# Layer B of a hybrid decoder step: keys and values turned by VectorE and on-chip transfers instead of by TensorE

## The reference

```python
qkv = h @ w_in[:, :3072]                      # 1024 tokens
conv = silu(sum(xpad[:, w:w + T] * conv_w[w] for w in range(4)))
q, k, v = split(conv)                         # (T, 8 heads, 128)
q, k = l2norm(q) * SCALE, l2norm(k)
kb   = k * beta
lmat = strict_lower(kb @ k.T) * decay         # in each chunk of tokens
sol  = triangular_solve(lmat, [v * beta, kb * exp(gc)])     # unit diagonal
u, w = sol
aqk  = (q @ k.T) * decay
kdec = k * exp(g_last - gc)
# chunk after chunk:
v_new = u - w @ S
o     = (q * exp(gc)) @ S + aqk @ v_new
S     = S * exp(gl) + kdec.T @ v_new
```

## Time and profile before

| | us |
|---|---|
| median of three runs | 2113.65 |
| the profiled execution: its own time | 2113.68 |
| the profiled execution: span from first to last instruction | 2111.6 |
| TensorE busy in the span | 2072.5 (98%) |
| VectorE, ScalarE, GpSimd busy | 997.2, 697.7, 454.6 |

### The profile page before, as it was taken

How to read it: one execution, slowest core, us unless ns; L and a number is a source line. 1 busy time by engine, 2 the same in 40 slices (tenths; PEclk the granted TensorE clock), 3 DMA queues, 4 the chain that set the end, 5 groups by cost and what they waited for, 6 DMA issues and landing times. The chain is left out here.

```text
span 2111.6 us, 36594 instructions
## 1 busy us (share of the span) xinstructions
PE 2072.5 (98%) x14446; PEld 1487.2 (70%) x14446; DVE 997.2 (47%) x2664; ACT 697.7 (33%) x1631; POOL 454.6 (22%) x639
## 2 busy tenths in 40 slices
PE   8999999999999999999999999999999999999998
PEld 6888888888888887555466777767666666665444
DVE  5234354354435345331238777777876133332252
ACT  4121321322131122231135555555564344532101
POOL 0522232222223213300023134322331200020000
PEclk9999999999999999999999999999998999999999
DMA  7411301211131127668412122222210461134451
GB/s 235 161 43 41 107 27 51 80 41 43 41 97 37 50 83 223 237 202 255 131 31 74 73 95 83 93 87 82 73 48 13 137 256 31 41 105 134 134 161 50
DMA packets 210238, 210.34 MB, mean 100 GB/s; under 512 B 14261, under 2 KB 181653, under 8 KB 209150
## 3 DMA queue, kind: packets, MB, share of 16 engines
q1 hardware_dynamic: 198070, 148.27, 23.7%
q0 software_dynamic: 12000, 59.73, 7.4%
HBM read 179.56 MB, written 68.23 MB: 117 GB/s over the span
## 5 line engine op out<-in xcount | busy, mean ns | idle before, releaser
L887 PE MATMUL bank<-arena 128*128 128x256 f32 (+1 forms) x2688 | 631.7, 386 | 0.0
L887 PEld LDWEIGHTS bank<-arena 128*128 128x128 f32 x2688 | 494.5, 190 | 75.3
L2104 PE MATMUL bank<-arena 128*128 128x352 f32 x1296 | 452.5, 470 | 0.1
L2104 PEld LDWEIGHTS bank<-arena 128*128 128x128 f32 x1296 | 220.8, 191 | 71.4 <-issue 1.0
L2909 PE MATMUL bank<-arena 128*128 128x352 f32 x576 | 176.4, 459 | 0.0
L3399 PE MATMUL bank<-arena 128*128 128x512 f32 x360 | 167.5, 599 | 0.0
L2162 PEld LDWEIGHTS bank<-arena 128*128 128x128 f32 x864 | 129.9, 194 | 45.7 <-DVE arena L2646 3.7
L2909 PEld LDWEIGHTS bank<-arena 128*128 128x128 f32 x576 | 106.6, 190 | 53.3
L1341 POOL TENSOR_TENSOR arena<-arena 128x272 f32<-128x272 f32 (+1 forms) x48 | 31.5, 656 | 507.4 <-ACT arena L1061 487.4
L2162 PE MATMUL bank<-arena 128*128 128x128 f32 x864 | 135.0, 280 | 1.5 <-DVE arena L2646 1.0
L1323 POOL TENSOR_TENSOR arena<-arena 128x512 f32<-128x512 f32 x96 | 122.8, 1279 | 11.3 <-POOL arena L1323 0.9
(11 more groups left out here) (432 smaller groups left out, 2754.1 us busy)
## 6 DMA issues: line engine op xcount, KB each, us to landing
arena<-in_w_in_a SPq DMA_DIRECT2D x48, 512.0 KB, 5.2
arena<-in_w_in_b SPq DMA_DIRECT2D x40, 512.0 KB, 7.5
arena<-in_cache_win_k SPq DMA_DIRECT2D x48, 256.0 KB, 6.1
arena<-in_cache_win_v SPq DMA_DIRECT2D x48, 256.0 KB, 4.7
out<-arena SPq DMA_DIRECT2D x40, 256.0 KB, 3.4
arena<-in_w_mem_kv SPq DMA_DIRECT2D x16, 512.0 KB, 8.1
arena<-in_cache_mem_k SPq DMA_DIRECT2D x32, 256.0 KB, 4.3
arena<-in_cache_mem_v SPq DMA_DIRECT2D x32, 256.0 KB, 4.2
```

The source lines that it names most:

```text
L887: m = nc.tensor.matmul(o[:, 0:hi - lo], w, y, start=k == 0 and i in (0, 1, 3, 5), stop=k == KH - 1, skip_group_check=i in (2, 4, 6))
L2104: m = nc.tensor.matmul(bank[j % 3][:, 0:PART], ring.slots[:, (B1 + b) % RING, k, :], part_in(k, part_), start=k == 0, stop=k == KD - 1)
```

## The change

VectorE turns the keys and the values inside 32x32 blocks by its stream transpose, one instruction of 128x512 each for k and v of a group (`kv_turned`); SyncE then issues 16 transfers for a group (`turned_to`), each of 32 partitions by 256 words (32 KB), that move the blocks between the quarters of the partitions and so complete the turn; ScalarE reads the result chunk by chunk and scales it into `kdec` and `vb` (`scale_turned`, two activations of 128x128 for a chunk, in slots 2 to 5 of iteration G for group G). VectorE's part for group G+1 is in slots 6 and 7 of iteration G; for group 0 it stands ahead of the loop. The steps "kt" and "vt" and their read-outs are gone. SyncE's order of weight loads is written anew around the transfers. In iteration 15 the four extra units move from slots 0 to 3 to slots 12 to 15. The buffers are parts of tensors that are free in this stage; the waits that guard them are in the diff. (The class `Chain` takes another way to its semaphore, which changes no instruction of the work.)

```diff
@@ names
+    turned_in = [brT[:, HB - 2, 0:1024]] * (2 * HB - 1) + [xpad[:, 0, 0:1024]]
+    turned_kv = [w.rearrange("p (b i c x) -> p b i c x", b=4, i=2, c=4) for w in turned_in]
+    kv_words = sb[:, ZM[0]:ZM[0] + 1024]
+    kv_back = kv_words.rearrange("p (a i c x) -> p a i c x", a=4, i=2, c=4)
-    PREP = {5: ("ra",), 7: ("kt",), 8: ("kk",), 9: ("qk",), 15: ("vt",)}
+    PREP = {5: ("ra",), 8: ("kk",), 9: ("qk",)}
+    AT_TURN = {6: 0, 7: 1}
+    SCALE_AT = {2: 0, 3: 1, 4: 2, 5: 3}
-    slots += [[(0, 1)] * 16, [(0, 2)] * 4 + [(0, 1)] * 12]
+    slots += [[(0, 1)] * 16, [(0, 1)] * 12 + [(0, 2)] * 4]
@@ SyncE
+        def turned_to(g):
+            sp.wait_ge(turnd, 2 * (g + 1))
+            after(sp, kvs, 4 * g)
+            for b in range(4):
+                for a in range(4):
+                    sp.dma_start(kv_words[quarter(b), 256 * a:256 * a + 256],
+                                 turned_in[g][quarter(a), 256 * b:256 * b + 256]).then_inc(kv_in[g % 2], 16)
+        for b in range(7):
+            weights(b)
+        turned_to(0)
+        for G in range(NG_):
+            if G % 2 and G < NG_ - 1:
+                weights(3 * (G // 2) + 8)
+                weights(3 * (G // 2) + 9)
+            if G + 1 < NG_:
+                turned_to(G + 1)
+            if G % 2 == 0:
+                weights(3 * (G // 2) + 7)
@@ TensorE
-                readout(pe, g, f"ks{c}" if c else "vt")
+                if c:
+                    readout(pe, g, f"ks{c}")
+                else:
+                    pe.wait_ge(kvs, 4 * g + 1)
+                pe.wait_ge(kvs, 4 * g + cl + 1)
                 to(g, f"su{c}", [(kdec[:, c, :], vn[:, c % 2, :])])
-            elif name == "kt":
-                to(G, "kt", [(ch(k_, c), None) for c in cs])
-            elif name == "vt":
-                to(G, "vt", [(ch(v, c), None) for c in cs])
@@ ScalarE
+        def scale_turned(g, cl):
+            w, c = hd[:, g // 2 % 2], GR[g % 2][0] + cl
+            if not cl:
+                act.wait_ge(kv_in[g % 2], 256 * (g // 2 + 1))
+                act.wait_ge(hdv, 3 * g + 3)
+                if g > 1:
+                    left(act, g - 2, f"su{GR[g % 2][1] - 1}")
+            wide = lambda v: v.rearrange("p (a x) -> p a x", x=32)
+            nc.scalar.activation(wide(kdec[:, c, :]), kv_back[:, :, 0, cl, :], ACT.Copy, scale=w[:, KD_, c:c + 1])
+            nc.scalar.activation(wide(vb[:, c, :]), kv_back[:, :, 1, cl, :], ACT.Copy,
+                                 scale=w[:, KN, c:c + 1]).then_inc(kvs, 1)
...
+                if G < NG_ and s in SCALE_AT:
+                    scale_turned(G, SCALE_AT[s])
                 for u in ended(units_at(G, s)):
                     piece(*u)
@@ VectorE
-            elif name == "kt":
-                dve.wait_ge(hdv, 3 * G + 3)
-                nc.vector.tensor_tensor(kdec[:, cs, :], bk(b), factors_of[:, KD_, cs]...)
-            elif name == "vt":
-                nc.vector.tensor_tensor(vb[:, cs, :], bk(b), factors_of[:, KN, cs]...)
+        def kv_turned(G, i):
+            h, gr = G // 2, G % 2
+            dve.wait_ge(sild, 3 * G + 2 + i)
+            if G and not i:
+                dve.wait_ge(kv_in[(G - 1) % 2], 256 * ((G + 1) // 2))
+            if G == NG_ - 1 and not i:
+                dve.wait_ge(cvd, 3 * NG_)
+                dve.wait_ge(tap, 3 * (NG_ - 2))
+            x = qkvT[:, h % 2, 1 + i, gr * 512:(gr + 1) * 512].rearrange("p (c b x) -> p c b x", c=4, b=4)
+            nc.vector.transpose(turned_kv[G][:, :, i].rearrange("p b c x -> p c b x"), x).then_inc(turnd, 1)
...
         turned(0, "qk")
+        kv_turned(0, 0)
+        kv_turned(0, 1)
         for w in range(CW):
             conv(1, 2, w)
...
                     chunk_step(G - 1, s)
+                if s in AT_TURN and G + 1 < NG_:
+                    kv_turned(G + 1, AT_TURN[s])
```

More of the change, by code:

```diff
@@ L115, with __init__ @@
 class Chain:
-    def __init__(self, nc, eng, name):
-        self.eng, self.sem, self.n = eng, nc.alloc_semaphore(name), 0
+    def __init__(self, sem, eng, name):
+        self.eng, self.sem, self.n = eng, sem(name), 0
     def __call__(self, ins):
@@ L525, in _ @@
     def _(dve):
-        own = Chain(nc, dve, "in_dve")
+        own = Chain(sem, dve, "in_dve")
         def norm(n):
@@ L1130, in _ @@
     def _(dve):
-        own = Chain(nc, dve, "dve_a")
+        own = Chain(sem, dve, "dve_a")
         def evacuate(t, i):
@@ L1300, in _ @@
     def _(pool):
-        own = Chain(nc, pool, "pool_a")
+        own = Chain(sem, pool, "pool_a")
         def weight_sums(pair, ns):
@@ L1747, in _ @@
     def _(dve):
-        own = Chain(nc, dve, "wa_dve")
+        own = Chain(sem, dve, "wa_dve")
         def add(n, half):
@@ L2000, in build @@
     (pd, pr_, wk, rd_act, rd_dve, cvd, sild, sqd, hdv, hda, exd, mt0, onm, sqo, fac, tails, sqrt_o, cstep, xzero,
-     cvs, spread, base, tap, chosen) = (
+     cvs, spread, base, tap, chosen, turnd, kv_even, kv_odd, kvs) = (
         sem(f"b_{n}") for n in (
@@ L2005, in build @@
             "out_factors", "conv_tails", "out_roots", "conv_steps", "buffers_zeroed", "samples_convolved",
-            "diagonals_spread", "base_steps", "first_taps", "blocks_chosen"))
+            "diagonals_spread", "base_steps", "first_taps", "blocks_chosen",
+            "kv_turned", "kv_moved_even", "kv_moved_odd", "kv_scaled"))
+    kv_in = (kv_even, kv_odd)
     s_out = stored["state"]
@@ L2078, in state_away, with weights @@
             sp.dma_start(p_delta[0, 0, h], S_of(h, NT)).then_inc(s_out, 16)
-        for b in range(3 * HB):
+        def turned_to(g):
[5 more added lines that the diff above has]
+                                 turned_in[g][quarter(a), 256 * b:256 * b + 256]).then_inc(kv_in[g % 2], 16)
+        def weights(b):
             if b % 3 == 2 and b // 3 >= 3:
@@ L2313, in gate_piece @@
                 act.wait_ge(ring.used, B2 + i + 1)
+            if i == 1 and part_ == 0:
+                act.wait_ge(kvs, 4 * NG_)
             if i == 2 and part_ == 0:
@@ L2390, in outputs @@
             b = left(act, g, "ot")
+            if g == 2 * (HB - 2):
+                act.wait_ge(kv_in[0], 256 * HB)
             nc.scalar.activation(brT[:, g // 2, g % 2 * 512:(g % 2 + 1) * 512], b[:, :], ACT.Copy,
                                  scale=onw).then_inc(rd_act, 1)
+        def scale_turned(g, cl):
[9 more added lines that the diff above has]
+                                 scale=w[:, KN, c:c + 1]).then_inc(kvs, 1)
         def choose_blocks(G):
@@ L2489, in _ @@
     def _(dve):
-        own = Chain(nc, dve, "b_dve")
+        own = Chain(sem, dve, "b_dve")
         stepped = [0]
@@ L2643, in chunk_step @@
             if x == "a" and c:
-                readout(dve, g, "vt")
+                dve.wait_ge(kvs, 4 * g + cl + 1)
                 b = left(dve, g, f"ks{c}")
@@ L2772, in _ @@
     def _(pool):
-        own = Chain(nc, pool, "b_pool")
+        own = Chain(sem, pool, "b_pool")
         def prefix(h, i):
@@ L3009, in _ @@
     def _(dve):
-        own = Chain(nc, dve, "m_dve")
+        own = Chain(sem, dve, "m_dve")
         def conv_turned(t):
@@ L3487, in _ @@
     def _(act):
-        own = Chain(nc, act, "d_act_own")
+        own = Chain(sem, act, "d_act_own")
         def squared(o):
@@ L3558, in _ @@
     def _(dve):
-        own = Chain(nc, dve, "wb_dve")
+        own = Chain(sem, dve, "wb_dve")
         gt2 = lambda v: v[:, 64:66].unsqueeze(2)
```

6 lines of the change are left out of this document (removed).

## The result

The changed kernel takes **2338.4 us** (median of 4 runs, 2336.44 to 2338.97) against 2112.92 (4 runs, 2111.94 to 2114.21) of the kernel before on the same chip: a ratio of 1.1065, interval 1.1046 to 1.1084. The forecast was 2107.1, in a range of 2099 to 2115. It was wrong, and by a cause that it had priced at nothing.

What follows compares the result with a forecast made beforehand. TensorE, busy 2072.5 of 2111.6 us, was taken to bound the kernel; -10.3 (steady) + 2.6 (iteration 0) - 0.1 (13, 14) + 1.2 (15) = -6.6 from 2113.7 gave 2107.1 us, range 2099 to 2115.

Steps and rivals of the forecast that it cites:

- The transfers in those iterations: Iterations 1 to 12: last landing 14 us after VectorE's second turn (bounds 7.2, 17.3), hidden in 24.6 us: 0.
- The slower rival: Each group's 16 transfers run one after another, 29.8 us against 24.6 of room: 3.7 lost per group, 2162; 8 in 100.
- Steady iterations: Iterations 1 to 12: TensorE spared 24 turns at 0.43 us, -10.3 us (bounds 5.2 and 10.3 gained).
- The exponentials' chain: Rival, steady part: ScalarE's added scalings delay exponentials and VectorE's kk read-out, losing half of 10.3: 2112.3 us; 13 in 100.
- Iteration 0: First loop iteration: ScalarE waits for transfers landing at 1128, x4 +3.0 us, "vt" returns 0.43: +2.6 (bounds +1.0, +4.6).
- The first group's stall and the clock: Rival, iteration 0: x4 5.0 us late, then a half-clock stretch; -6.6 + 2.0 + 5.6 gives 2114.7 us; 13 in 100.
- Iterations 13 and 14: Late iterations where units run out: almost nothing gained, half clock counted as it was: -0.1 us (bounds -1.7, +1.0).
- Iteration 15: Last iteration: moved units and ScalarE's scalings make TensorE stand 1.7 us more, less 0.43: +1.2 (bounds -0.9, +2.6).

Runs made afterwards that it cites:

- the half transfers: Changed kernel, cache copies as they were, each of the 16 transfers carrying 128 of 256 words a partition: 2337.02 us (one run).
- the copies spread: Changed kernel with each two-row cache copy written as two one-row copies, each seen as 16 pieces: 2110.56 us, ratio 0.9989 to the kernel before.

## Why the prediction was wrong, step by step

**The step that failed** is "The transfers in those iterations", priced at 0 because landing 14 us behind the turn, at worst 17.3, would be hidden in a room of 24.6. The room was right, and in quiet the landing too (11 to 14 us). The bound was not: beside a copy the first group's last transfer landed 44 us behind the turn, and the later ones up to 59. It came from the stores of a state, 11.6 us at most, and from the median of the weight loads, 9.9. A median over loads that meet a copy and loads that don't is no bound, and the trace of before had the right number one view further on. The weight loads by line, from 1106 to 1560 us, in the kernel before:

```profile
L139 SPq DMA_DIRECT2D arena<-in_w_in_b x20: 367/368/2649, 1144.7 to 1559.0; - x20
...
DMA to landing us min/median/max: 4.1/10.8/43.5
```

Five of these loads were issued together with the first copy of a pair, at 1156.9, 1224.6, 1292.7, 1360.8 and 1429.0, and landed 42 to 43.5 us later, while the second ran. Nothing waited for it, since the ring of four blocks asks for a block over an iteration ahead. The change put a wait with 24.6 us of room onto the same queue. The DMA share in the earlier trace rows said the rest: 0.22 for 79 GB/s in the loop, and from 1134 to 1144 us, where nearly a copy alone runs, in the kernel before:

```profile
1134.00:1144.00 10.00, 9.59 (x119) 6.17 (x112) 7.68 (x15) 4.74 (x10) 2.67 (x3) 1.00 0.13 54
```

That is two engines full and fourteen empty: a transfer that is spread over all sixteen is as late as its share on those two. I had counted bytes ("as many bytes as the 16 together"), and the half transfers show that bytes are not what counts.

The Trainium skill states these parts (DMA: Bandwidth & Descriptors): that an engine takes turns between queues packet by packet ("Queues, rings and completion order"), that each engine posts its own share of the completion and that the slowest dimension of a copy sets how many engines it uses ("Why a DMA increments its semaphore by 16 and not by 1"). All three agree with the runs here: 16 packets against 16, fourteen landings within 3.1 us and two after 33 and 34, and a share of 0.12 for a copy whose slowest dimension is 2. Taking turns sounds fair; with 65 KB on one side and 1 KB on the other it is a wait of 2.4 us for each small packet.

**The slower rival had the right sign and the wrong reason.** It let the transfers follow one another, at 3.7 us lost in each of 15 groups, 2162. In quiet they don't: without copies ScalarE waits for them in the first group alone, and SyncE issues all 16 in 10 to 12 us. (The 2 us of the Trainium skill that stand beside this rival are given there for transfers that GpSimd issues; these are SyncE's and land after 1.8 to 1.9 us, their issues overlapping.) Its aside, "more beside the copies", was the matter, and it had no number.

**Steady iterations.** The stream transpose of 128x1920 (`base_rows`; L2617 before, L2669 after) stands once ahead of the loop and then in slot 11 of each iteration, so its starts mark the periods. From iteration 0 to iteration 12 the kernel before takes 1547.21 - 1139.52 = 407.69 us, the changed one without copies 1538.39 - 1139.99 = 398.40. The rows of the latter:

```profile
1117.04 2.17 DVE L2669 STREAM_TRANSPOSE arena<-arena 128x1920 f32<-128x1920 f32 x1
...
1139.99 2.17 DVE L2669 STREAM_TRANSPOSE arena<-arena 128x1920 f32<-128x1920 f32 x1
...
1538.39 2.17 DVE L2669 STREAM_TRANSPOSE arena<-arena 128x1920 f32<-128x1920 f32 x1
...
1569.12 2.18 DVE L2669 STREAM_TRANSPOSE arena<-arena 128x1920 f32<-128x1920 f32 x1
...
1597.45 2.17 DVE L2669 STREAM_TRANSPOSE arena<-arena 128x1920 f32<-128x1920 f32 x1
```

So 9.3 us are gained in twelve periods, against 10.3: 33.20 each instead of 33.97. (The 34.47 and 33.6 of the prediction come from one period, longer than their mean.) The exponentials' chain did not become the pace.

**Iteration 0**: without copies ScalarE waits 7.06 us for the transfers and x4 stands 2.20; the stretch between the first two of these marks grows from 21.64 to 22.95, +1.3. x4 starts at 1131.18, 0.47 later than before, though VectorE's read-outs in front of the loop came 1.37 earlier in this run: +1.8. Forecast were +2.6, and +3.0 for x4. The path was right; ScalarE went on at 1125.68, in the old kernel's time 1127.05, where I took 1128.

**The first group's stall and the clock**, a rival with 13 in 100, is borne out in part: in the profiled executions 2.2 us of standing left the clock at 1.00, and 4.0 and 5.0 us had a clock of 0.61 and 0.67 behind them. The rival gave it 5.6 + 2.0; iteration 0 took 4.2 and 4.3 us more in these two than where x4 stood 2.2, the longer standing counted in. The rest of the 7 us between the bands is not the first group's (see the table above).

**Iterations 13 and 14**: forecast -0.1; they took 30.73 and 28.33 us instead of 31.05 and 29.83, so -1.8, a bit past my near bound. x6 of iteration 13 does stand 1.87 instead of 1.74, and still the whole got shorter. Most of this is the clock, which the prediction counted "as it was": from 1565 to 1600 it was 0.90 instead of 0.80. With the copies spread it was 0.80 again, and iteration 14 took 29.67 us, 0.2 less than before. **Iteration 15**: from the mark in iteration 14 to the loop's last transposes 66.05 us instead of 65.05, +1.0 against +1.2; moving the units alone gives +1.3 there.

**Sum.** Without the copies the change gives 2102.58 - 2112.39 = -9.8 us, and -11.4 against the kernel before without copies, where the terms came to -6.6. The profiled executions differ by 9.6: -0.8 before the first mark, +1.3, -9.3, -1.8 and +1.0. Against the terms that is 1.3 less in iteration 0, 1.7 less in iterations 13 and 14 (mostly clock), 0.8 less ahead of the loop, where no term stood and where the clock differs as well (0.86 against 1.00 from 1050 to 1075), and 1.0 more in the steady part. So the main term was near, and part of the rest was not the change's own. The term that was missing is +235.8.

## What to carry to other kernels

A new wait on a transfer is judged by the longest landing among the transfers of its queue while the big copies run, not by their median, and its room is held against the 25 to 45 us of a whole copy. A DMA share that is a small whole number of sixteenths beside few GB/s says that a copy fills few engines, and that what is spread over all of them may wait on those; cut the copy so that it spreads before putting anything tight beside it. Moving work off the busiest engine then paid what the timelines had said, and the first group, which has no cover, was better left as it was (2103.76 against 2110.56 and 2108.35). Landings of transfers that share a semaphore are told apart by count alone: only the last of them is what it says.

## What the runs showed of the hardware

- A copy of two rows of 1 MB in main memory keeps two DMA engines busy and moves 53 GB/s; the same bytes as two copies of one row land in about 7 us each. The kernel before takes the same time with the spread copies (ratio 1.0003) and with none (1.0005).
- Behind such a copy SyncE's issues of small transfers took up to 12.1 us each, instead of 0.59.
- A packet of 65 KB takes 2.4 us on its engine, and one packet of a transfer inside the core's memory goes past for each. The weight loads wait like this as well: two of the kernel before, issued at 1144.7 and 1150.6 beside a copy that landed at 1157.6, landed 14.2 and 9.9 us later, at 1158.9 and 1160.5. Most of their turns let one packet of 512 bytes past (two against the copy's two from 1154.3 to 1156.7), but not all: the DMA view from 1149 to 1152.2 us has 79 against 3. Why some go in bundles and others singly stays open.

```profile
q0 software_dynamic: 3, 0.20, 14.2%
q1 hardware_dynamic: 79, 0.04, 7.5%
```

- A transfer of 32 KB inside the core's memory lands in 1.8 to 1.9 us in quiet (least and median), and its issue takes SyncE 0.59 us, against 0.36 for a store of 128 partitions.
